# Latent attention on one core: rotary halves of the queries exchanged by partition-shifted VectorE writes instead of a permutation matmul

## The reference, cut to what matters

```python
def apply_rope(x, cos, sin):
    half = x.shape[-1] // 2
    x1, x2 = x[..., :half], x[..., half:]
    return jnp.concatenate([x1 * cos - x2 * sin, x2 * cos + x1 * sin], axis=-1).astype(x.dtype)

def mla_mixer(xn, cos, sin, w_in, q_norm, w_q_up, kv_norm, w_kv_up, w_out):
    ...
    q = (rms_norm(q_lat, q_norm) @ w_q_up).reshape(B, S, N_HEADS, QK_NOPE_DIM + QK_ROPE_DIM)
    q_nope = q[..., :QK_NOPE_DIM]
    q_rope = apply_rope(q[..., QK_NOPE_DIM:], cos[:, :, None, :], sin[:, :, None, :])
    ...
    o = causal_block_attention(q_nope, q_rope, k_nope, k_rope, v)
    return (o.reshape(B, S, D_INNER) * jax.nn.silu(z)) @ w_out
```

## Time and profile before

| | |
|---|---|
| time, median of 3 runs | 2243.41 us (2237.18, 2245.2, 2243.41) |
| the profiled execution's own time | 2249.47 us |
| its span, first to last instruction | 2247.7 us |
| TensorE busy | 2191.1 us, 97% of the span |
| VectorE, ScalarE, GpSimd busy | 1071.0, 949.0, 1068.0 us (48%, 42%, 48%) |
| mean granted TensorE clock | 0.986 |
| attention stage of the latent block | about 880 to 1110 us of the span |

### The profile page before, as it was taken

The page is one execution under the profiler, slowest core; times in us unless marked ns, Lnnn a source line. Parts: engine busy times, 40 slices in busy tenths (PEclk is TensorE's granted clock), DMA queues, the critical chain, the costliest instruction groups (busy, mean ns, idle before and its releaser), DMA issues.

```text
span 2247.7 us, 33240 instructions
## 1 busy us (share of the span) xinstructions
PE 2191.1 (97%) x10952; PEld 1767.8 (79%) x10952; DVE 1071.0 (48%) x1486; ACT 949.0 (42%) x1641; POOL 1068.0 (48%) x787
## 2 busy tenths in 40 slices
PE   8999999999999999999999999999999998999996
PEld 6788888888888887777788788887778676888885
DVE  6842224445442262555426822337577437666412
ACT  4243334343443443444333244434545545444422
POOL 5654444544444444444345654444331433555553
PEclk9999999999999999999999999999999899999998
DMA  4233323233333332211132233233220022332332
GB/s 139 94 103 94 103 84 103 94 95 101 93 102 95 99 93 94 65 58 57 38 99 88 92 103 95 94 100 99 76 76 3 1 66 66 102 93 93 103 103 103
DMA packets 53791, 194.33 MB, mean 86 GB/s; under 512 B 6096, under 2 KB 6352, under 8 KB 53712
## 3 DMA queue, kind: packets, MB, share of 16 engines
q1 hardware_dynamic: 52704, 191.13, 27.0%
q10 hardware_dynamic: 1008, 2.14, 0.3%
HBM read 191.14 MB, written 2.10 MB: 86 GB/s over the span
## 4 chain that ended last, share of the span: by engine, by line
PE 48%; issue 30%; POOL 18%; DVE 2%; ACT 1%; POOLq 1%; ACTq 0%; DVEq 0%
POOL w_lo L601 18%; PE proj L672 11%; PE proj L674 11%; PE proj L673 11%; PE aux L814 2%; PE proj L839 2%; PE proj L768 1%; PE proj L770 1%; PE proj L769 1%; PE aux L817 1%; PE aux L825 1%; PE proj L937 1%; PE aux L937 1%; PE proj L1067 0%; DVE cy L2040 0%
## 5 line engine op out<-in xcount | busy, mean ns | idle before, releaser
L601 POOL TENSOR_TENSOR w_lo<-w_stage,w_hi 128x512 fp32r<-128x512 f32 x716 | 989.2, 1387 | 1011.9 <-ACT w_hi L1286 1011.0
L1286 ACT ACTIVATE w_hi<-w_stage 128x512 fp32r<-128x512 f32 x716 | 442.4, 628 | 841.6 <-PE proj L674 766.7
L672 PE MATMUL proj<-xh,w_hi 128*128 128x512 f32 x1696 | 668.6, 394 | 4.5 <-POOL w_lo L601 4.5
L674 PE MATMUL proj<-xh,w_lo 128*128 128x512 f32 x1696 | 660.8, 390 | 0.0
L673 PE MATMUL proj<-xl,w_hi 128*128 128x512 f32 x1696 | 660.8, 390 | 0.0
L672 PEld LDWEIGHTS proj<-xh,w_hi 128*128 128x128 f32 x1696 | 318.6, 188 | 82.4 <-POOL w_lo L601 12.9
L673 PEld LDWEIGHTS proj<-xl,w_hi 128*128 128x128 f32 x1696 | 318.9, 188 | 67.2 <-issue 2.4
L674 PEld LDWEIGHTS proj<-xh,w_lo 128*128 128x128 f32 x1696 | 318.8, 188 | 67.1
L672 PE MATMUL proj<-act_h,w_hi 128*128 128x512 f32 (+1 forms) x840 | 327.2, 390 | 0.2 <-POOL w_lo L601 0.2
L673 PE MATMUL proj<-act_l,w_hi 128*128 128x512 f32 (+1 forms) x840 | 327.0, 389 | 0.0
L674 PE MATMUL proj<-act_h,w_lo 128*128 128x512 f32 (+1 forms) x840 | 326.8, 389 | 0.0
(11 more groups left out here) (340 smaller groups left out, 2321.7 us busy)
## 6 DMA issues: line engine op xcount, KB each, us to landing
w_stage<-stream SPq DMA_DIRECT2D x358, 512.0 KB, 3.5
out<-x_res SPq DMA_DIRECT2D x3, 512.0 KB, 2.6
x_res<-x SPq DMA_DIRECT2D x2, 512.0 KB, 8.2
consts_sb<-consts ACTq DMA_DIRECT2D x1, 640.0 KB, 3.9
x_res<-x ACTq DMA_DIRECT2D x1, 512.0 KB, 7.2
out<-x_res SPq DMA_DIRECT2D x2, 256.0 KB, 2.0
x_res<-x SPq DMA_DIRECT2D x1, 256.0 KB, 3.3
x_res<-x ACTq DMA_DIRECT2D x1, 256.0 KB, 5.1
```

The source lines that it names most:

```text
L601: pool.tensor_tensor(w_lo[:, at, :], w_stage[:, at, :], w_hi[:, at, :].bitcast(F32), ALU.subtract).then_inc(stage_free, 1)
L672: pe.matmul(o, w_hi[:, slot, cols], hi, start=(b == 0), stop=False)
L674: mm = pe.matmul(o, w_lo[:, slot, cols], hi, start=False, stop=(b == blocks - 1))
L1286: act.activation(w_hi[:, u % RING, :], w_stage[:, u % RING, :], ACT.Copy).then_inc(hi_done, 1)
```

## The change

The permutation product of the queries goes, with its place in the list of up tiles, and so does `take_swap`. `take_rope` now makes the exchange itself: four multiplications, each on 32 partitions, read one group of 32 partitions of the rope tile and of `sn` and write the product to the partner group of `q_sin`; then come the product with `cs` and the sum of the two, and only the sum counts the tile as taken. The counts of `up_taken` fall from six to five for each pair.

```diff
@@ up_tiles
-        for kind, ends in (("q0", 1), ("q1", 1), ("rope", 1), ("k0", 0), ("swap", 0), ("k1", 1)):
+        for kind, ends in (("q0", 1), ("q1", 1), ("rope", 1), ("k0", 0), ("k1", 1)):
@@ TensorE
-                def swap_up():
-                    j = next(ups)
-                    up_free(pe, j)
-                    pe.matmul(up_bank(j), con("swap", P), q_sin[:, :], start=True, stop=True).then_inc(up_done, 1)
-
...
                     if qb == 0:
-                        pe.wait_ge(up_taken, 6 * p + 6)
+                        pe.wait_ge(up_taken, 5 * p + 5)
...
                     k_up(0)
-                    swap_up()
                     k_up(1)
...
-                pe.wait_ge(up_taken, 6 * HEAD_PAIRS)
+                pe.wait_ge(up_taken, 5 * HEAD_PAIRS)
@@ VectorE
                 def take_rope(p):
                     b = next_up()
-                    link(dve.tensor_tensor(q_sin[:, :], b, sn[:, :], ALU.mult))
-                    took(dve.tensor_tensor(qr[:, p % 2, :], b, cs[:, :], ALU.mult))
-
-                def take_swap(p):
-                    took(dve.tensor_tensor(qr[:, p % 2, :], qr[:, p % 2, :], next_up(), ALU.add))
+                    for g in range(4):
+                        to, of = slice(32 * g, 32 * g + 32), slice(32 * (g ^ 1), 32 * (g ^ 1) + 32)
+                        link(dve.tensor_tensor(q_sin[to, :], b[of, :], sn[of, :], ALU.mult))
+                    link(dve.tensor_tensor(qr[:, p % 2, :], b, cs[:, :], ALU.mult))
+                    took(dve.tensor_tensor(qr[:, p % 2, :], qr[:, p % 2, :], q_sin[:, :], ALU.add))
...
                     normalise(p, 3)
                     if more:
-                        take_swap(p + 1)
                         take_k(p + 1, 1)
```

More of the change, by code:

```diff
@@ L1988, in latent_attention @@
                 take_k(0, 0)
-                take_swap(0)
                 take_k(0, 1)
```

## The result

The changed kernel took **2253.07 us** (median of 20 runs, 2247.44 to 2263.7) against 2241.4 us of the kernel before (20 runs, 2233.89 to 2247.39). The ratio is 1.0053, with a 95% interval of 1.0039 to 1.0067: some 12 us longer (8.7 to 15.0). The prediction said 2260, 16.8 us longer, and a range of 2249 to 2267. The direction, the mechanism and the range hold; the size was some 5 us too large, and the experiments show which terms were off. (The other 2 us between 2260 and 2253.07 lie in the time of the kernel before, put at 2243.41 then from three runs.)

The account below looks back on a forecast made before the run. TensorE, busy throughout the attention stage, was taken as the bound. First pair 1.9, loop pairs 5.3, first pair's clock fall 1.6 and loop clock falls 8.0 made 16.8 us over 2243.41: 2260 us, range 2249 to 2267.

Parts of the forecast that it names:

- the mechanism: In each loop pair VectorE's longer rotary block makes fourth maximum 1.89 us late; TensorE waits 1.8 us for ScalarE's copy.
- The first pair: Start of the stage: k1 waits for the rotary tile's bank, v tiles 1.9 us later; one clock fall, 1.6 us.
- The price of a 32-partition multiplication: In VectorE's rotary block: 0.72 us from start to start for each; lower bound 0.18 us.
- The second rival: In VectorE's rotary block: multiplications on 32 partitions are shorter, 7.4 us gained, 2236 us; chance 0.06.
- The loop pairs: Seven pairs after the first: the third block's value products start 0.75 us later in each, 5.3 us.
- The clock: Loop pauses in the stage: five of seven lose TensorE's full clock, at 1.6 us each, 8.0 us.
- the prediction's likeliest case: Loop pauses in the stage: four to seven of seven lose the clock, 2258.6 to 2263.4 us; chance 0.62.
- first rival: Loop pauses of 1.8 us: the clock holds in all or all but three, 2251 to 2257 us; chance 0.20.
- The third rival: Rotary block: VectorE's sum costs 1.14 us more in eight blocks, all seven loop pauses lose clock, 2272 us; chance 0.09.

Follow-up runs that it names:

- e1: Changed kernel with one sine multiplication on 128 partitions in place of the four on 32, exchange left out: 2239.95 us, ratio to before 1.0002.
- e4: Changed kernel with the exchange made by four ScalarE copies, VectorE subtracting after k1's copy, first rotary tile in its own bank: 2233.98 us, ratio 0.9974.
- e3: Changed kernel with two of the four multiplications made twice, six in all: 2271.55 us, ratio to before 1.014.
- e7: e6 with its multiplications in the order of groups 1, 0, 2, 3: one profile, a pair takes 28.53 us.
- e6: Changed kernel with each of the four multiplications writing the partitions it reads, so nothing is exchanged: profiles only, a pair takes 28.41 us.
- e2: Changed kernel with the sum moved back behind k0's copy, the tile counted as taken at the cosine product: 2249.2 us, ratio to before 1.0041.
- the last experiment with ScalarE: e4 with the last pair's VectorE subtraction moved ahead of k1's copy: 2232.42 us, ratio to before 0.9956.

## Why the prediction was right, and where its size was off

- **The mechanism holds, step by step.** The mask follows the sum with no idle time, ScalarE's copy is late, TensorE waits seven times 1.76 to 1.80 us for it (predicted 1.8), and once 3.10 us (predicted 3.2) in the first pair. The 1.8 agree a little better than they should: the prediction counted from start to start at a pace of 0.23 us, and so counted the pause is 949.64 - (947.48 + 0.23) = 1.93 us. Taking three multiplications away ended the loss (e1), taking VectorE out of the exchange turned it into the full gain (e4), and adding two cost two (e3).
- **The price of a 32-partition multiplication** was right: 687 ns, from start to start 0.72. The second rival is out; what the Trainium skill states (page "Vector Engine (DVE) Microarchitecture Reference", section 3.8, as the prediction cites it) agrees with the trace, since the write to a partner group added nothing (687 ns, and 685 without it).
- **The first pair**: 1.9 + 1.6 = 3.5 us were predicted, the measured A grew by 3.41, with the clock at 0.50 behind the pause.
- **The loop pairs: 0.75 was predicted, 1.01 measured**, so 7.1 us instead of 5.3. Two small things were missing. The first multiplication starts 0.45 us after the normalisation's start, not 0.33 (935.51, below, to 935.84 before): that is the hold of e7. From there to the mask it is then 4.34 us, as 6 x 0.72 says, and the maximum is late by (945.51 - 940.72) - (938.27 - 935.51) = 2.03 us instead of 1.89. And the third block's values take 1.45 us to the next product (949.64 to 951.09) instead of 1.34 (943.55 to 944.89): 0.75 + 0.14 + 0.11 = 1.00. Why they take longer behind a pause was not tried. The normalisation in the kernel before:

```profile
935.51 0.42 DVE L1968 TENSOR_SCALAR pr<-pr,small 128x384 f32<-128x384 f32 x1
```

- **The clock is the step that failed in size.** Five of seven falls were assumed, 8.0 us, by placing 1.8 us between a pause of 1.30 us that held and one of 2.24 us that fell. Three profiles show two, one and one, so 1.65 to 3.3 us. The price of a fall, 1.6, was right (1.67). Two single pauses in another part of the program were taken to say what one of 1.8 us does; that fell 4 of 28 times. And the pause of 2.24 us says less than it was taken for: it stands behind the stage in all twelve profiles, 2.24 us long in each, and lost the clock in nine of them and kept it in three. One of the three is the changed kernel's first profile, where the matmuls behind it go on at 0.23 us from start to start (below). So the prediction's likeliest case, four to seven falls, did not come in; its first rival, with three at most, did (2251 to 2257 us, and 2253.07 lies there). That the forecast came as near as it did is in part luck: the clock was priced 4.7 to 6.4 us too dear and the pairs 1.8 us too cheap, and the two partly cancel.

```profile
1125.49 0.50 PE L847 MATMUL proj<-act_h,w_hi 128*128 128x512 f32 x1 [2.24 <-DVE act_l L1974]
1125.83 0.40 PE L848 MATMUL proj<-act_l,w_hi 128*128 128x512 f32 x1
1126.07 0.39 PE L849 MATMUL proj<-act_h,w_lo 128*128 128x512 f32 x1
```

- **The rule on the clock that the prediction set beside its rows.** The Trainium skill (page "TensorE: Matmul & The Clock Gate", section "Why this matters for your kernels") warns of gaps over about 3 us. The trace doesn't agree: pauses of 1.8, 2.24 and 2.45 us lost the clock in part of the cases.
- **The sum again**, with one fall in the loop as two of three profiles have it: 3.4 + 7 x 1.01 + 1.65 = 12.1 us. Measured were 11.9 and 12.1 in the stages of those two profiles, 13.7 in the one with two falls, and 11.7 between the medians of the runs.
- **The third rival's mechanism exists, but not here.** The sum is stretched beside GpSimd's `w_lo` when it meets it (1.53 us in e1), and the changed kernel's multiplications move it past that, as the prediction said from GpSimd's idle time.

## What to carry to other kernels

A product taken off a full TensorE is worth its time only if the engine that takes the work over isn't, at that place, the one that TensorE waits for next. Averages said that VectorE had room (15.3 of 27.5 us); once the product was gone, the 1.02 us of idle time ahead of one maximum was all the room there was. Ask who else is idle there: ScalarE was, for 4 us, and with the exchange on it the same idea gains 0.4% instead of losing 0.5%.

Instructions on VectorE go by elements for each partition (687 ns on 32, 684 on 128): splitting a 128-partition instruction into four of 32 costs four instructions. And when several pauses stand close to what costs the clock elsewhere, price them by a chance and not by a threshold.

## What was not expected of the hardware

- A VectorE instruction that begins on other partitions than the one before starts 0.11 us later (0.45 against 0.34 us), seen in the changed kernel, e6 and e7.
- VectorE's sum of two SBUF tiles and GpSimd's work on SBUF lengthen one another: the sum to 1.53 and 1.8 us (e1, e4), or GpSimd's normalisation from 1.85 to 2.37 us (e2). Which of the two gives way was different in e1 and e2, though in both GpSimd's row starts first (0.28 and 0.34 us before). And they don't always meet: in e4 VectorE's product of two SBUF tiles ran beside the last 0.7 us of GpSimd's normalisation, and neither was longer than elsewhere. This was not followed up.

```profile
940.05 0.69 DVE L1957 TENSOR_TENSOR q_sin<-q_sin,sn 128x512 f32<-128x512 f32 x1
...
938.94 1.86 POOL L619 TENSOR_SCALAR pr<-pr,small 128x512 f32<-128x512 f32 x1 [4.03 <-DVE small L1978]
```

- ScalarE's copy of 32 partitions to partner partitions takes as long as its copy of 128 from PSUM, 587 and 598 ns, less than VectorE's multiplication (687). The groups of the last experiment with ScalarE:

```profile
L1416 ACT ACTIVATE q_sin<-proj 32x512 f32<-32x512 f32 x28 | 16.4, 587 | 3.5 <-DVE qr L1953 3.3
...
L1408 ACT ACTIVATE v_heads<-proj 128x512 f32<-128x512 f32 x16 | 9.6, 598 | 9.3 <-PE proj L797 9.3
```

- The same pause in the same kernel loses the clock in one execution and not in the next (pair 5 of the changed kernel, and the pause of 2.24 us behind the stage). In the stage that made 1.7 us between executions of the same kernel; most of the spread between its three profiles lies behind the stage, in a part that took 1121.7 to 1129.9 us.
